# Overflow quads behind one flag and one branch per engine, in a mixture-of-experts kernel on one core

## The reference, cut to what matters

```python
def grouped_moe(h, router_w, router_bias, w1, w3, w2):
    ...
    _, e_idx = lax.top_k(jnp.where(e_mask, sel, -jnp.inf), TOP_K)
    gate = jnp.take_along_axis(scores, e_idx, axis=1)
    gate = gate / jnp.sum(gate, axis=-1, keepdims=True)
    ...
    def expert_block(args):
        xb, e = args
        return (jax.nn.silu(xb @ w1[e]) * (xb @ w3[e])) @ w2[e]
    ...
```

## Time and profile before

| what | value |
|---|---|
| median of 3 runs | 2013.21 us (2007.89 to 2017.04) |
| the profiled execution's own time | 2005.7 us |
| its span, first to last instruction | 2003.9 us |
| PE busy | 1638.2 us (82%) |
| DVE busy | 738.6 us (37%) |
| ACT busy | 258.5 us (13%) |
| bytes moved by DMA | 574.99 MB, mean 287 GB/s |

### The profile page before, as it was taken

How to read it: one execution, slowest core, us unless ns; L and a number is a source line. 1 busy time by engine, 2 the same in 40 slices (tenths; PEclk the granted TensorE clock), 3 DMA queues, 4 the chain that set the end, 5 groups by cost and what they waited for, 6 DMA issues and landing times.

```text
span 2003.9 us, 25262 instructions
## 1 busy us (share of the span) xinstructions
PE 1638.2 (82%) x10030; PEld 980.6 (49%) x10031; DVE 738.6 (37%) x1498; ACT 258.5 (13%) x630; POOL 94.0 (5%) x125
## 2 busy tenths in 40 slices
PE   5999988766756588976666657989999999999998
PEld 3754553222222155322222215766996485669963
DVE  2865462111101027211110114974466313444662
ACT  1002210000000012000000002332110122311100
POOL 1001001000000001930000000000000000000000
PEclk9999998988787789988787879999999999999999
DMA  9989479999999996999999996204435364204351
GB/s 363 399 331 414 171 300 414 421 421 422 422 422 422 410 380 259 379 405 421 422 422 422 422 403 261 85 17 163 168 127 216 115 246 153 100 11 168 127 211 41
DMA packets 121814, 574.99 MB, mean 287 GB/s; under 512 B 10724, under 2 KB 15176, under 8 KB 67064
## 3 DMA queue, kind: packets, MB, share of 16 engines
q1 hardware_dynamic: 119552, 567.63, 70.7%
q0 software_dynamic: 1104, 2.86, 0.5%
q10 hardware_dynamic: 1064, 3.17, 0.4%
HBM read 578.88 MB, written 1.05 MB: 289 GB/s over the span
## 4 chain that ended last, share of the span: by engine, by line
PE 42%; DMA 32%; PEld 9%; DVE 8%; issue 4%; ACT 2%; SPq 1%; PEldq 1%; DVEq 1%; ACTq 0%
DMA ring_buffer<-in_exp_w 29%; PE ps L1488 7%; PE ps L2213 6%; PE ps L2184 6%; PEld ps L2184 5%; PE ps L1513 4%; PE ps L2902 4%; PE ps L2013 3%; DMA ring_buffer<-in_ada_w 2%; PEld ps L831 2%; PE ps L1004 1%; PE ps L2893 1%; PE ps L2155 1%; SPq L1375 1%; PEld ps L2155 1%
## 5 line engine op out<-in xcount | busy, mean ns | idle before, releaser
L1488 PE MATMUL ps<-ring_buffer,arena 128*32 128x512 f32 x1984 | 291.0, 744 | 164.4 <-DMA ring_buffer<-in_exp_w 161.8
L1488 PEld LDWEIGHTS ps<-ring_buffer,arena 128*32 128x32 f32 x1984 | 75.6, 133 | 366.8 <-issue 309.7
L1513 PE MATMUL ps<-ring_buffer,arena 128*32 128x512 f32 x1088 | 151.4, 708 | 88.1 <-DMA ring_buffer<-in_exp_w 77.0
L1684 DVE TENSOR_TENSOR arena<-arena,ps 128x512 f32<-128x512 f32 x18 | 19.1, 1063 | 395.8 <-PE ps L1488 395.8
L2184 PE MATMUL ps<-arena,ring_buffer 128*128 128x128 f32 x1152 | 133.9, 276 | 3.7 <-issue 3.7
L2184 PEld LDWEIGHTS ps<-arena,ring_buffer 128*128 128x128 f32 x1152 | 130.8, 192 | 5.7 <-issue 5.7
L1513 PEld LDWEIGHTS ps<-ring_buffer,arena 128*32 128x32 f32 x1088 | 40.6, 127 | 187.2 <-issue 146.6
L2213 PE MATMUL ps<-ring_buffer,arena 128*128 128x512 f32 x252 | 111.0, 594 | 3.4 <-issue 2.3
L2184 PE MATMUL ps<-hT,ring_buffer 128*128 128x128 f32 x864 | 99.4, 275 | 0.0
L2184 PEld LDWEIGHTS ps<-hT,ring_buffer 128*128 128x128 f32 x864 | 97.9, 192 | 0.0
L1702 DVE TENSOR_TENSOR arena<-ps,gates 128x512 f32<-128x512 f32 x16 | 11.1, 693 | 195.1 <-PE ps L1513 195.1
(11 more groups left out here) (573 smaller groups left out, 2062.2 us busy)
## 6 DMA issues: line engine op xcount, KB each, us to landing
ring_buffer<-in_exp_w SPq DMA_DIRECT2D x376, 1024.0 KB, 17.1
ring_buffer<-in_ffn_w SPq DMA_DIRECT2D x30, 2048.0 KB, 13.8
ring_buffer<-in_ada_w SPq DMA_DIRECT2D x24, 2048.0 KB, 18.0
ring_buffer<-in_c_w_in SPq DMA_DIRECT2D x8, 2048.0 KB, 12.6
ring_buffer<-in_attn_w_in SPq DMA_DIRECT2D x6, 2048.0 KB, 16.5
arena<-in_exp_w SPq DMA_DIRECT2D x6, 1024.0 KB, 8.0
ring_buffer<-in_ab_w_in SPq DMA_DIRECT2D x3, 2048.0 KB, 14.2
ring_buffer<-in_ffn_w SPq DMA_DIRECT2D x6, 1024.0 KB, 6.9
```

The costliest lines, as they stand in the source:

```text
L1488: ins = pe.matmul(ps[c, bank, :], tokens[:, 4 * phase + k, c], halves[j][:, k, :], start=(phase == 0 and k == 0), stop=(phase == 1 and k = ...
L1513: ins = pe.matmul(ps[c, bank, :], tokens[:, 2 * phase + k, c], halves[j][:, k, half * 512:(half + 1) * 512], start=(phase == 0 and k == 0) ...
```

## The change

The four numbers of `quad_live` become one flag, `any_overflow`, which is up if the first overflow block has an expert. Each engine reads it once. If it is up, the loop over the four overflow quads runs inside the If, and every quad in it is worked on, those with no tokens too (their transfers are left out by `cond`, as those of dead blocks in a live quad were before). If it is not, a single Else counts every semaphore up by four times its count. In `table_dve` the places behind the overflow follow from all four quads or from none (`lives`), which takes one operation instead of three. The rest of the kernel is the same.

```diff
-            quad_live = take(2, QUADS - FIRST_QUADS, dt=I32)[:, layer]
+            any_overflow = take(2, 1, dt=I32)[:, layer]
...
-                v(dve.tensor_scalar(lives, more_end[:, N_EXPERTS - 1:N_EXPERTS], 1.0 / QUAD, 0.5 - 0.5 / QUAD, ALU.mult, ALU.add))
-                v(dve.tensor_scalar(lives, lives, ROUND, None, ALU.add))
-                v(dve.tensor_scalar(lives, lives, -ROUND, float(P), ALU.add, ALU.mult))
+                v(dve.tensor_scalar(lives, more_end[:, N_EXPERTS - 1:N_EXPERTS], 0.5, float(P * MORE_QUADS), ALU.is_ge, ALU.mult))
...
-                with sp.Fori(0, MORE_QUADS) as i:
-                    quad_is_live = sp.value_load(quad_live[0:1, bass.ds(i, 1)], min_val=0, max_val=1)
-                    with sp.If(quad_is_live > 0):
+                overflows = sp.value_load(any_overflow[0:1, :], min_val=0, max_val=1)
+                with sp.If(overflows > 0):
+                    with sp.Fori(0, MORE_QUADS) as i:
...
-                    with sp.Else():
-                        sp.wait_ge(more_used, m0 + RING + UNITS * i)
-                        for slot in range(RING):
-                            sp.drain().then_inc(more_landed[slot], 64)
-                        sp.drain().then_inc(more_used, UNITS)
+                with sp.Else():
+                    sp.wait_ge(more_used, m0 + RING)
+                    for slot in range(RING):
+                        sp.drain().then_inc(more_landed[slot], 64 * MORE_QUADS)
+                    sp.drain().then_inc(more_used, UNITS * MORE_QUADS)
...
-                with eng.Fori(0, QUADS - FIRST_QUADS) as more:
-                    live = eng.value_load(quad_live[0:1, bass.ds(more, 1)], min_val=0, max_val=1)
-                    with eng.If(live > 0):
+                overflows = eng.value_load(any_overflow[0:1, :], min_val=0, max_val=1)
+                with eng.If(overflows > 0):
+                    with eng.Fori(0, MORE_QUADS) as more:
                         quad(more, more + FIRST_QUADS, overflow=True)
-                    with eng.Else():
-
-                        for s, count in signals:
-                            eng.drain().then_inc(s, count)
-                        if steps:
-                            eng.drain().then_inc(quad_step, steps)
+                with eng.Else():
+
+                    for s, count in signals:
+                        eng.drain().then_inc(s, count * MORE_QUADS)
+                    if steps:
+                        eng.drain().then_inc(quad_step, steps * MORE_QUADS)
```

More of the change, by code:

```diff
@@ L1321, in table_dve @@
                 v(dve.tensor_scalar(table[:, 0, :], block_expert, float(N_EXPERTS - 1), None, ALU.min))
-                v(dve.tensor_scalar(quad_live, block_expert.rearrange("p (q j) -> p q j", j=QUAD)[:, :, 0],
-                                    float(N_EXPERTS), None, ALU.is_lt))
+                v(dve.tensor_scalar(any_overflow, block_expert[:, 0:1], float(N_EXPERTS), None, ALU.is_lt))
                 dve.tensor_scalar(table[:, 1, :], block_expert, float(N_EXPERTS), None, ALU.is_lt).then_inc(table_ready, 1)
```

## The result

The changed kernel took 1999.63 us (median of 7 runs, 1996.1 to 2003.58), the kernel before 2009.51 us beside it (7 runs, 2007.89 to 2017.04). The ratio is 0.9947, with a 95% interval of 0.9923 to 0.997. The forecast was -0.17%, within half a percent; measured were -0.53%. So the kernel became faster by some 0.4 to 0.5%, 8.6 to 10.7 us, where 3.4 us had been worked out. About 3 us of the distance to the forecast are in its base: the median of the first three runs, 2013.21 us, was high; 35 more runs of the kernel before gave 2010.66 us.

The account below looks back on a forecast made before the run. The prediction took DMA of expert weights to bound the two expert stages. Only the two closed dips counted, 1.35 and 2.05 us, together 3.4 us: 2013.2 - 3.4 = 2009.8 us, -0.17%, range 2002.5 to 2016 us.

Parts of the forecast that it names:

- (a): PE's dead path: three of four loop iterations go, 6.8 us a layer; quad 7 opens at 671.7 and 1169.4 us.
- (b): DMA queue at quad 7: SP issues at 678.3 and 1176.3 us, both dips close, together 3.4 us.
- (c): SP's own overflow loop: SP reaches quad 7's loads 5.5 us sooner, but the DMA is full: nothing.
- (d): DVE and ACT: both leave their overflow loops ahead of PE, so nothing.
- (e): The table on DVE: two operations fewer, 0.4 us a layer; taken as nothing, 0.8 us if on the path.
- (f): Live path, a loop inside the If: not entered, with 28 drains of 28.
- late-code rival: PE waits for quad 7's code: once, 6.1 us a layer, 2011.8 us or more, chance 0.13; twice, 2024.0 us, 0.03.
- The stall is on the path in full: Rival: PE's stalls ahead of quad 7 bound both layers; 13.6 us would go, 1999.6 us; chance 0.07.

Follow-up runs that it names:

- the experiments with 63, 96 and 180 drains: The changed kernel with 63, 96 or 180 more drains on PE's dead path in each layer; ratios to the kernel before 0.9958, 0.9976 and 1.0022.
- the two part kernels: The kernel before with the short dead path on PE alone, ratio 0.9959, or on SP, ACT and DVE only, ratio 1.0003.
- the added loop: The kernel before with a second dead loop on PE behind the first, 16 iterations in each layer, jumping over 122 filling matmuls; no measured time given.
- the filling matmuls ahead of the loop: The kernel before with 12 pairs of filling matmuls queued on PE ahead of the overflow loop; ratio 1.003.
- 13 pairs of filling matmuls: The kernel before with 13 in place of 10 pairs of filling matmuls at the head of the pooling stage; ratio 0.9998.

## Why the prediction was wrong

**What it had right.** (a) PE opened quad 7 at 671.07 us, 671.7 forecast; in layer 1 after 5.39 us of idle time, 5.7 forecast. (b) in its mechanism: SP's first issue at 678.06, no dip in either layer; the experiments with 63, 96 and 180 drains put the point at which the queue runs dry between 10.1 and 12.7 us of idle time, where step (b) had 5.7 + 5.7 = 11.4. (c) and (d): the other engines' part measured 1.0003. The fewer table operations of (e) were in neither of the two part kernels; the changed kernel's 0.9957 against 0.9959 with PE's part alone leaves room for its 0.8 us and doesn't show it. (f): seven drains per layer, the flag was never up. Neither late-code rival came: the one jump took 6.0 to 6.3 us, with no second long one, in all of the profiles with the short path on PE (7.2 us in one layer of the execution whose clock was 0.64).

**The step that failed** stands near the end of (b): "From the last landing of quad 7 on, PE's tail and all that follows start that much sooner". It takes for granted that the parts behind keep their lengths, and they don't: TensorE's half-clock stretches fell otherwise there. The table has the means over five profiles with a long dead path on PE (before four times, and the short path on the others) and five without dips (changed twice, PE alone, 63 drains, no overflow code). All times are differences of rows of PE's timeline.

| us | long | short | difference |
|---|---|---|---|
| ahead of the first expert matmul | 268.0 | 267.9 | 0.1 |
| layer 0: first expert matmul to last down-projection | 452.4 (452.6) | 451.0 | 1.4 (1.6) |
| quad 7's tail in layer 0 | 8.7 | 9.3 | -0.6 |
| pooling stage | 48.1 | 44.5 | 3.6 (3.5) |
| layer 1: first expert matmul to last down-projection | 441.5 (443.2) | 438.4 | 3.1 (4.8) |
| quad 7's tail in layer 1 | 8.7 (8.9) | 9.6 | -0.9 (-0.7) |
| the rest of the kernel | 778.2 (778.6) | 779.7 | -1.5 (-1.1) |
| span | 2005.6 (2008.0) | 2000.5 | 5.1 (7.5) |

In brackets, where it differs, stands the mean of all five long profiles, without brackets that without the execution that had the second long branch. The two dips themselves were sized well: 3.4 us forecast, and 1.4 us measured in layer 0. Of layer 1's 3.1 us a part goes with a half-clock stretch of 3.4 us that starts between 799 and 808 us, which the two profiles of the changed kernel lack (436.9 us). The three short kernels that have it took 439.4 us, 2.1 less than the long ones; the forecast had 2.05. The pooling stage gave 3.6 us that the forecast hadn't. Half clock takes up 10.2 us of it in each of the five long profiles, in one piece or in two, and 3.4 us in each of the five short ones, so 6.8 us less, worth 3.4 us of full-clock work. The tails took 1.5 us back. In layer 0 the half-clock stretch stands at the same place, 714.6 to 721.4 us before and 714.7 to 721.5 us after, while the last down-projection starts at 718.71 us before and 716.93 us after, so that more of the tail fell into it. These sums make 5.1 us, 7.5 with the brackets, against the 8.6 to 10.7 measured.

**The rivals.** "The stall is on the path in full" named the time nearest to the measured one, 1999.6 us, and is yet refuted, by the kernel without overflow code and by the 63 drains: 10.1 us of standing still cost no more than 5.5 or 0.9. That the number fits is chance: it came from the base of 2013.2 us, which was some 3 us high, and from 13.6 us that the runs don't show. A second long branch does exist, but in the kernel before, and there in a later iteration of the loop. The prediction took each of these iterations to cost 2.27 us in every run.

**What stays open.** Of the measured gain 1 to 6 us are not in the profiles' sums, and the sums are rough: the two executions of the changed kernel alone lie 8.2 us apart (1994.3 and 2002.5 us), 5.2 of them ahead of the first expert matmul. The kernel before took over 2012 us in 38 of its 127 runs of all sets. The kernels with a single branch or none, and no more idle time than before, did so in one of 75 (2013 us, with 96 drains). A long branch like that of 9.70 us would do that, but it was seen once in 14 dead loops of four iterations, and in none of 60 later iterations of the added loop. How often it comes in the timed runs is not known, so this share of the gain is argued and not shown. Nor do I know why the clock falls in the pooling stage in one order of events and not in another. The longer half clock there went with an opening of quad 7 after 12.5 to 12.8 us of idle time, and after 11.2 us with the filling matmuls ahead of the loop; it came neither after 10.1 us and less nor after 18.6, and once, in the profile with 13 pairs of filling matmuls, it was absent after 12.7.

## What to carry to other kernels

Here a stall of one engine beside a full DMA queue cost nothing measurable until it outlasted the queue, and about two thirds of itself in the expert stages from that point on. To find such a point, look for slices in which the DMA share falls below full behind it, read the margin from the issuing queue's last and next issue, and test it with idle time put in. In this kernel with its half-clock stretches the parts behind the changed place didn't keep their lengths (-1.5 to +3.6 us a part): give them a range of a few microseconds of their own, in both directions. And take more than one profile of the kernel before, and more than three runs, before half a percent is forecast.

## What the runs showed of the hardware

The first taken jump over the overflow quad's code, or over the 122 matmuls of the added loop, took 5.9 to 6.5 us on PE in every profile (but for 7.2 us in one layer of the execution whose clock was 0.64, and for L1438 in layer 1 of the kernel with the added loop, 0.33 us in both executions), and later ones 0.21 us; once a later one took 9.70 us. The Trainium skill, "Runtime: NRT & Kernel Launch", section "Instruction fetch mechanics", says that a taken branch out of the window of code now held has to wait for a fetch of its target. The first jumps and the short repeats agree with that. Whether the 9.70 us was such a fetch, no run shows. A drain on PE that signals nothing took 0.07 us in a row (4.5 us for 63), one that signals 0.11 us.
